# Moving state products, a wait and a gather in the stretch before the expert products of a one-core decoder layer

## The reference

```
x   = layernorm(x)
mix, C, n, m, S = mixer(x, states)        # mLSTM and HGRN2 heads; new states are outputs
x   = layernorm(ALPHA * x + mix)          # the "second norm" below
logits = x @ w_router + b_router          # top 4 of 32 experts, softmax over the four
gate = min(xb @ wg[e] + bg[e], 7); up = clip(xb @ wu[e] + bu[e], -7, 7)
y   = ((up + 1) * gate * sigmoid(1.702 * gate)) @ wd[e] + bd[e]
x   = layernorm(ALPHA * x + sum of gated y + ple)
S_prompt = sum over tokens of k^T v (decayed); C_prompt and n_prompt likewise
```

## Time and profile before

| what | value |
|---|---|
| time before, median of 3 runs | 1250.95 us (1250.07 to 1252.32) |
| the profiled execution's own time | 1253.7 us |
| its span in the profile | 1251.8 us |
| PE busy | 1169.6 us (93%) |
| DVE, ACT, POOL busy | 357.2, 186.4, 69.7 us |
| read from HBM | 436.54 MB, mean 353 GB/s with the 4.73 MB written |
| chain that ended last | PE 73%, DMA 17%, DVE 7%, ACT 2% |

### The profile page before, as it was taken

One profiled execution on the slowest core, in us unless ns is written; L12 is line 12 of the kernel. 1 busy time (PEld: TensorE's weight loads), 2 busy tenths in 40 slices (PEclk: granted clock), 3 DMA queues, 4 the chain that ended last, 5 costly groups with the idle time before them and its releaser, 6 DMA issues.

```text
span 1251.8 us, 13175 instructions
## 1 busy us (share of the span) xinstructions
PE 1169.6 (93%) x5601; PEld 485.4 (39%) x5601; DVE 357.2 (29%) x568; ACT 186.4 (15%) x346; POOL 69.7 (6%) x74
## 2 busy tenths in 40 slices
PE   5999999899999997899999999999999999998985
PEld 4678775633333332243333333332323232322221
DVE  6866334531313130111222222122212121213014
ACT  2444342311001010020201000010101010110000
POOL 3100141110101030000000000000000000000000
PEclk9999999699999998999999999999999999999988
DMA  9652130689999999999999999999999999999892
GB/s 313 215 151 68 68 139 19 264 350 380 420 421 421 421 418 386 420 421 422 416 421 420 421 421 421 405 421 421 420 421 421 419 422 413 421 421 421 357 421 86
DMA packets 70509, 442.18 MB, mean 353 GB/s; under 512 B 7952, under 2 KB 8368, under 8 KB 21296
## 3 DMA queue, kind: packets, MB, share of 16 engines
q1 hardware_dynamic: 65600, 425.66, 83.5%
q0 software_dynamic: 4848, 15.64, 3.7%
HBM read 436.54 MB, written 4.73 MB: 353 GB/s over the span
## 4 chain that ended last, share of the span: by engine, by line
PE 73%; DMA 17%; DVE 7%; ACT 2%; issue 1%; SPq 1%; DVEq 0%
PE ps L1011 42%; DMA ring<-in_w_up 12%; PE ps L593 9%; PE ps L992 6%; DMA ring<-in_w_gate 4%; PE ps L944 3%; DVE y_s L1883 3%; PE ps L814 2%; DVE h_s L1881 2%; PE ps L999 2%; PE ps L621 1%; ACT hTe L1162 1%; PE ps L1027 1%; PE ps L976 1%; PE ps L948 1%
## 5 line engine op out<-in xcount | busy, mean ns | idle before, releaser
L1011 PE MATMUL ps<-ring,xTe 128*64 128x512 f32 x1536 | 358.1, 601 | 17.7 <-DMA ring<-in_w_up 14.5
L1011 PEld LDWEIGHTS ps<-ring,xTe 128*64 128x64 f32 x1536 | 105.5, 136 | 242.4 <-issue 242.2
L1011 PE MATMUL ps<-ring,hTe 128*64 128x512 f32 x768 | 180.8, 610 | 7.1 <-DMA ring<-in_w_down 7.1
L1863 DVE TENSOR_TENSOR xs<-xs,ps 128x512 f32<-128x512 f32 x64 | 44.0, 688 | 348.5 <-PE ps L992 348.4
L593 PE MATMUL ps<-xT,ring 128*128 128x288 f32 x448 | 115.4, 414 | 1.0 <-PE ps L593 0.6
L1011 PE MATMUL ps<-more,xTe 128*64 128x512 f32 x496 | 113.5, 599 | 1.6 <-DMA more<-in_w_up 0.8
L1011 PEld LDWEIGHTS ps<-ring,hTe 128*64 128x64 f32 x768 | 52.3, 139 | 121.8 <-issue 121.4
L593 PEld LDWEIGHTS ps<-xT,ring 128*128 128x128 f32 x448 | 84.8, 193 | 25.3 <-issue 2.3
L992 PE MATMUL ps<-y_s,GT 128*128 128x512 f32 (+1 forms) x256 | 82.5, 520 | 2.2 <-ACT y_s L1162 1.2
L1881 DVE TENSOR_SCALAR h_s<-ps 128x512 f32<-128x512 f32 x32 | 21.8, 681 | 161.0 <-PE ps L1011 161.0
L1162 ACT ACTIVATE h_s<-g_s 128x1024 f32<-128x1024 f32 x16 | 16.9, 1056 | 307.7 <-DVE g_s L1871 307.7
(11 more groups left out here) (371 smaller groups left out, 817.8 us busy)
## 6 DMA issues: line engine op xcount, KB each, us to landing
ring<-in_w_gate SPq DMA_DIRECT2D x96, 1024.0 KB, 11.2
ring<-in_w_up SPq DMA_DIRECT2D x96, 1024.0 KB, 11.7
ring<-in_w_down SPq DMA_DIRECT2D x96, 1024.0 KB, 13.6
more<-in_w_gate SPq DMA_DIRECT2D x32, 1024.0 KB, 9.9
more<-in_w_down SPq DMA_DIRECT2D x32, 1024.0 KB, 13.0
more<-in_w_up SPq DMA_DIRECT2D x30, 1024.0 KB, 13.1
ring<-in_w_in SPq DMA_DIRECT2D x28, 512.0 KB, 6.2
ring<-in_w_out SPq DMA_DIRECT2D x8, 512.0 KB, 5.1
```

Of the source, the lines that this page charges most:

```text
L1011: last = mm(ps[64 * q:64 * q + 64, bank0 + half, :], lhs(k, q), wide(t)[:, k % 2, half * 512:(half + 1) * 512], start=False, stop=k == KT - 1)
L1863: tt(x, x, ps[:, CB_BANKS[n], 0:512 if i < 2 else QW], ALU.add).then_inc(S["cb_added"], 1)
```

## The change

Six edits in one stretch of the program:

1. `prompt_states_b` moves on TensorE from behind `sample_ranks` to between `row_stats(2)` and `transpose_normed(2)`. Its wait for `kbt_ok` goes, since TensorE waits for the same value a little earlier.
2. VectorE's wait for `kbt_mm`, which stood before the whole norm of tile 1, stands at that norm's last step alone.
3. ScalarE's `norm_scale(1, 5)` moves ahead of the three copies of keys (`KBt`).
4. VectorE's `select` is split into `top_experts` and `chosen`; `chosen(0)` stands behind tile 2's statistics, and `rest_of(1, 0)` behind tile 2's norm. ScalarE's `part(2, 0)` goes ahead of `part(1, 1)`, and the counts of `later_rest_ok` follow.
5. The second couple's gather moves from the first up products to the first gate products (still k = 1 and 3); ScalarE's copies of it move ahead of `copy_gates` and `swish`.
6. The first gather writes banks 7 and 2 instead of 0 and 1, and the gate products start after one copied half of `xTe` instead of two; the wait for the second half stands behind step k = 3.

```diff
--- before.py
+++ after.py
@@ -825,7 +825,6 @@
                 last.then_inc(S["st_mm"], 1)
 
             def prompt_states_b():
-                pe.wait_ge(S["kbt_ok"], 3)
                 for h in range(H):
                     for i in range(2):
                         last = mm(ps[:, 5, h * DV:(h + 1) * DV], KBt[:, i, h * P:(h + 1) * P],
@@ -917,13 +916,13 @@
             pe.wait_ge(S["kbt_ok"], 3)
             transpose_normed(1)
             row_stats(2)
+            prompt_states_b()
             transpose_normed(2)
             route(1)
             route(2)
             prompt_ranks()
             sample_rows()
             sample_ranks()
-            prompt_states_b()
             prompt_states_a()
 
             def ple_product(n, u):
@@ -1032,9 +1031,16 @@
 
             def beside_gate(p, k):
 
+
                 if p == 0:
+                    if k in (1, 3):
+                        if k == 1:
+                            pe.wait_ge(S["OH_ok"], 1)
+                            pe.wait_ge(S["st_ok"], 2)
+                        gather(xTe[0], 2 * (k - 1), 4, 4 + k // 2, 128, 128)
+                    if k == 3:
+                        pe.wait_ge(S["xTe_ok"], 2)
                     if k == 5:
-                        pe.wait_ge(S["st_ok"], 2)
                         pe.wait_ge(S["GW_ok"], 1)
                         gates_to_rows(6)
                     if k == 6:
@@ -1072,9 +1078,6 @@
             def beside_up(p, k):
 
 
-                if p == 0 and k in (1, 3):
-                    pe.wait_ge(S["OH_ok"], 1)
-                    gather(xTe[0], 2 * (k - 1), 4, 4 + k // 2, 128, 128)
                 if p < GATHERS and k == 5:
                     later_rows(p, 0)
                 if k in (1, 4) and STATE_PAIR0 <= p < STATE_PAIR0 + N_STATES // PER_PAIR:
@@ -1093,12 +1096,12 @@
             pe.wait_ge(S["part_ok"], 8)
             pe.wait_ge(S["OH_first"], 1)
             for n in range(2):
-                gather(xTe[0], 4 * n, 4, n, 0, 128)
+                gather(xTe[0], 4 * n, 4, ROW_BANKS[n], 0, 128)
             for p in range(NPAIR):
                 if p == 1:
                     pe.wait_ge(S["pos_ok"], 1)
                     extra = pe.value_load(n_exti[0:1, 0:1], min_val=0, max_val=NXP)
-                pe.wait_ge(S["xTe_ok"], (2, 4)[p] if p < 2 else 4 + 8 * (p // 2))
+                pe.wait_ge(S["xTe_ok"], (1, 4)[p] if p < 2 else 4 + 8 * (p // 2))
                 pe.wait_ge(S["sel_ok"], p + 1)
                 lhs = x_cols(xTe[p // 2 % 2], 128 * (p % 2))
                 products(p, 0, 0, lhs, 0, sel[p % 2], lambda k: beside_gate(p, k), S["gate_mm"])
@@ -1292,7 +1295,7 @@
             def part(i, q):
 
                 if q:
-                    act.wait_ge(*((S["rest_ok"], q), (S["later_rest_ok"], q), (S["later_rest_ok"], 2 + q))[i])
+                    act.wait_ge(*((S["rest_ok"], q), (S["later_rest_ok"], 2 * q - 1), (S["later_rest_ok"], 2 * q))[i])
                 else:
                     act.wait_ge(S["x_norm"], 4 + i)
                 if i < 2:
@@ -1315,6 +1318,7 @@
             part(0, 1)
             copy_xT(0, 6, 0)
             part(0, 2)
+            norm_scale(1, 5)
             act.wait_ge(S["kbt_mm"], 1)
             for i, (_, r) in enumerate(TILES):
                 f(KBt[0:r, i, :], ps[0:r, KEY_BANKS[i], :], ACT.Copy).then_inc(S["kbt_ok"], 1)
@@ -1334,12 +1338,11 @@
                 f(gate[0:r, i, :], top_v[0:r, i, 0:TOPK], ACT.Exp, bias=neg_v[0:r, i:i + 1],
                   accum_out=gsum[0:r, i:i + 1]).then_inc(S["gate_exp"], 1)
 
-            norm_scale(1, 5)
             part(1, 0)
             copy_xT(1, 6, 0)
             norm_scale(2, 6)
+            part(2, 0)
             part(1, 1)
-            part(2, 0)
             copy_xT(2, 6, 0)
             part(2, 1)
             part(1, 2)
@@ -1378,7 +1381,7 @@
                 f(y_s[:, :], ps[:, 4:6, :].rearrange("p b n -> p (b n)"), ACT.Copy).then_inc(S["y_ok"], 1)
 
             for n in range(2):
-                copy_rows(n, xTe[0][:, 4 * n:4 * n + 4, 0:128], ps[:, n, :])
+                copy_rows(n, xTe[0][:, 4 * n:4 * n + 4, 0:128], ps[:, ROW_BANKS[n], :])
             for p in range(NPAIR):
                 if p == 1:
                     act.wait_ge(S["pos_ok"], 1)
@@ -1392,11 +1395,10 @@
                             f(ple[:, i, 0:w], ple[:, i, 0:w], ACT.Sigmoid).then_inc(S["ple_sig"], 1)
                 else:
                     for n in range(2):
+                        copy_rows(2 + n, xTe[0][:, 4 * n:4 * n + 4, 128:256], ps[:, 4 + n, :])
+                    for n in range(2):
                         copy_gates(n, 6 + n)
                 swish(p)
-                if p == 0:
-                    for n in range(2):
-                        copy_rows(2 + n, xTe[0][:, 4 * n:4 * n + 4, 128:256], ps[:, 4 + n, :])
                 for n in range(4):
                     if p < GATHERS:
                         k = 4 * (p % 2) + n
@@ -1469,6 +1471,8 @@
                 dve.wait_ge(S["ln_std"], n)
                 step(nc.vector.reciprocal(mv[:, i, 3:4], mv[:, i, 2:3]))
                 if 4 <= n < 6:
+                    if n == 5:
+                        dve.wait_ge(S["kbt_mm"], 1)
                     last = stt(x1[:, i, :].rearrange("r (k p) -> r k p", k=KT), by_step(x), mv[:, i, 3:4], by_step(b),
                                ALU.mult, ALU.add)
                 else:
@@ -1787,7 +1791,6 @@
                 tt(KAt[0:r, i, :].rearrange("p (h d) -> p h d", h=H), src.rearrange("p (h d) -> p h d", h=H),
                    cols[0:r, i, 1, :].unsqueeze(2).to_broadcast([r, H, DKA]), ALU.mult).then_inc(S["kat_ok"], 1)
             mixer_residual(1)
-            dve.wait_ge(S["kbt_mm"], 1)
             norm(1, 5)
             def rest_of(i, q):
 
@@ -1798,7 +1801,7 @@
                     dve.wait_ge(S["partq_ok"], q + 1)
                     tt(rest_q[:, :], rest_q[:, :] if q else x1q[:, :], xbq[:, q, :], ALU.subtract).then_inc(S["later_rest_ok"], 1)
 
-            def select(i):
+            def top_experts(i):
 
                 dve.wait_ge(S["router_mm"], i + 1)
                 tt(logit[:, :], ps[:, ROUTE_BANKS[i], 0:NE], br[:, :], ALU.add).then_inc(S["logits_ok"], 1)
@@ -1806,23 +1809,28 @@
                 step(nc.vector.max(top_v[:, i, :], logit[:, :]))
                 step(nc.vector.max_index(top_i[:, i, :], top_v[:, i, :], logit[:, :]))
                 step(nc.vector.tensor_copy(top_f[:, i, :], top_i[:, i, :]))
+
+            def chosen(i):
                 step(tt(oneh[:, i, :, :], iota.unsqueeze(1).to_broadcast([P, TOPK, NE]),
                         top_f[:, i, 0:TOPK].unsqueeze(2).to_broadcast([P, TOPK, NE]), ALU.is_equal))
                 nc.vector.tensor_reduce(pick[:, i, :], oneh[:, i, :, :].rearrange("p k e -> p e k"),
                                         axis=AX_X, op=ALU.add).then_inc(S["pick_ok"], 1)
 
-            select(0)
+            top_experts(0)
             mixer_residual(2)
             tile_stats(2)
             spread_stats()
-            rest_of(1, 0)
+            chosen(0)
             norm_stats(2, 6)
             norm_apply(2, 6)
+            rest_of(1, 0)
+            rest_of(2, 0)
             rest_of(1, 1)
-            rest_of(2, 0)
-            select(1)
+            top_experts(1)
+            chosen(1)
             rest_of(2, 1)
-            select(2)
+            top_experts(2)
+            chosen(2)
 
             dve.wait_ge(S["rank_mm"], 1)
             step(tt(row_of[:, :, 0:NE], ps[:, RANK_BANK, P:P + 3 * NE].rearrange("p (i e) -> p i e", i=3), pick[:, :, :], ALU.mult))
```

## The result

| | before | changed |
|---|---|---|
| median of 6 runs each | 1251.82 us (1250.07 to 1254.13) | 1244.54 us (1241.18 to 1246.65) |
| profiled execution, its span | 1253.7 us, 1251.8 us | 1243.77 us, 1241.9 us |
| first gate product of pair 0 (T0) | 248.34 us | 240.37 us |

The two medians are 7.3 us apart. The ratio of the comparison is 0.9932, with a 95% interval of 0.9919 to 0.9945: 8.5 us faster, between 6.9 and 10.1. It equals the mean of the changed kernel over the mean of the three later runs of before (1254.13, 1253.08 and 1251.32 us); the three earlier ones, from which the prediction started, lie lower. The forecast was 1243.3 us, 7.6 us faster, so it held in sign, and the median came out 1.2 us above it.

A forecast was written before the change was run, and what follows sets the result against it. The prediction took the restart of the weight stream, 4.21 us after T0, as the bound. Terms of 3.7 (states b), 3.9 (norm, router) and 0.7 (copy), less 0.7 (gather), gave 7.6: 1250.95 - 7.6 = 1243.3 us, range 1238.0 to 1247.0.

The forecast's parts named there:

- The bound: Weight stream: DMA engines are full at 418 to 421 GB/s, so only their idle time before it can be won.
- The norm: VectorE's norm of tile 1 starts 2.43 us earlier; together with a router partly at full clock, a term of 3.9 us.
- States b: State products b, put before tile 2's transposes, take 1.9 us hidden in a wait; 3.7 us go from behind the ranks.
- The new wait: Before tile 2's router, TensorE waits for ScalarE's copy until 225.9; 1.2 us of the gain is lost.
- The clock: TensorE's clock falls near 226.2 at tile 2's router and returns at 238.0, 4.6 us after states a begin.
- the term of a gather partly at half clock: First gather before the gate products: 18% of it runs at half clock, taking 0.7 us off the gain.
- The copy: ScalarE's copy between first gather and first gate product no longer delays that product: a term of 0.7 us.
- The second gather: Second couple's gather in the gate products: costs nothing, covered by the 2.1 us DMA gap before 293; uncovered, up to 1.8 us.
- The stream: Weight tiles: ten are there before the restart at T0 + 4.2, 244.9, so all 7.6 us reach the stream.
- Rival 1: TensorE's clock holds through the router: T0 12.9 us earlier, at 235.4, time 1238.0 us; chance 0.20.
- Rivals 2 and 3: 2: gain eaten in stream, low clock through gather, 1249.2 us, chance 0.10; 3: gate products start at half clock, 1256.7, 0.04.
- rival 2: Gain eaten by later releases (1.8 us), low clock through the gather (4.5 instead of 7.6), pair 0's work last: 1249.2; chance 0.10.

## Why the prediction was right, point by point

1. **The bound.** Right. The stream runs at the same 418 GB/s, and the shift of T0 is found again, within 0.3 us, at 1094.8.
2. **The norm.** Right: tile 1's transposes begin without waiting for the norm, the `lnq` product at 220.41 (forecast 220.1), tile 2's transposes at 222.52 (222.5).
3. **States b.** Right: from 220.66, 2.03 us, hidden. Putting it back cost 3.1 us in T0, 3.6 without what arose ahead of the edit, against the term of 3.7. The prediction did not ask what else states b does there: without it the clock fell 4.2 us sooner, counted from the same start.
4. **The new wait.** Right: 1.15 us before tile 2's router against 1.2, ended by ScalarE's copy. It lies at 224.61 to 225.76, so it ends 0.1 us before the forecast.
5. **The clock.** The fall was right, the rise and the length of states a were not. It fell at 226.1 (forecast 226.2) and came back at 236.4 (forecast 238.0), 3.2 us after states a had begun at 233.15, where I had taken 4.6 out of 3.4 to 5.6. So the term of a gather partly at half clock was 0 and not -0.7. The gather itself began 0.4 us late: states a with its sums took 4.05 us and not 3.4, because the 3.4 were read where the clock had risen half-way (240.94 to 244.32 holds the rise at 242.8). The two misses have opposite signs, and T0 moved by 7.97 and not 7.6. That the rise came in time is luck. In the five profiled executions with this order on TensorE it came 2.9 to 3.9 us after states a began in four and 9.0 in one (the restart held back), whose T0 was 3.0 us later for it. No rule that I used gives this; the span of 3.4 to 5.6 was too narrow on both sides.
6. **The copy.** Right: the first gate product waits for nothing, and 0.69 us return when it must wait for both halves.
7. **The second gather.** Right: no change, and the later gap shrank from 2.5 to 1.4 us as cover.
8. **The stream.** The sum was right; the step "the time goes with the restart at 252.55" failed in its place. The restart can come 2.3 us later relative to T0, and most issues of the later pairs move by 0.3 to 0.6. What did not move from T0 is the release by the first down step, at T0 + 43.8. Both move with T0 in the change, so the number did not suffer, and only the experiment told them apart.
9. **The rivals.** Rival 1 did not come in the changed kernel, but it is a state of this program: with wide fillers, or with states a early and one wide product, the clock held in the profiled execution, in the latter with nearly the T0 that was worked out. Rivals 2 and 3 did not come; the clock was back before the gather. But the low clock through the gather, a part of rival 2, did come in the profiled execution with the restart held back.

The median came out 1.2 us above the forecast though T0 moved by 0.4 us more than forecast. The forecast took its 7.6 us off 1250.95, the median of three runs; the three later runs of the same kernel have 1253.08, and all six 1251.82. The gain itself, 7.3 us between the medians of six and 8.5 by the ratio, lies on both sides of the 7.6 forecast and of the 7.97 by which T0 moved. The changed kernel's own runs are spread over 5.5 us, so a miss of 1.2 tells nothing more.

## What to carry to other kernels

Where a saturated stream of weights follows a serial start, look for the release that the stream cannot do without (here one step of TensorE, not the first restart), and count only what moves that. Float32 work of wider products, such as the state products here, that may stand anywhere is worth trying in the waits before a run of narrow ones: states b cost nothing there, and with it the clock fell 4 us later. What the clock then does differs from one execution to the next, so such a gain is read from many runs and not from one trace. A gap before the places were full, or one that merely handed work from one group of products to the next, was worth nothing here, however large it looked in the slices.

## What the runs showed of the hardware

- TensorE busy 17.00 of 17.00 us, 13.4 of them with narrow products, stood at a granted clock of 0.50; with some wide ones among them, busy 17.50 of 17.50 us, it stood at 1.00. The medians are 6.9 us apart.
- Useless wide products did not cost: with 4.8 us of them T0 came 1.5 us sooner in the profiled execution, and the runs lay within 0.75 us (five runs) instead of 5.5 (six).
- The same instructions can meet the clock's rise at very different times: 2.9 to 3.9 us after states a began in four profiled executions, 9.0 in a fifth, which put T0 3.0 us later.
- One program can scatter widely: with the key wait put back it took 1242.3 to 1253.3 us. Late drops of 3.4 or 6.8 us at half clock went with 1.9 us between two profiled spans, where the change edits nothing.
